# Second mixer (S5): rows on 128 partitions, turns by small diagonal products, copies shared between ScalarE and VectorE in another way

## The reference, cut to what matters

```python
h = modulate(rms_norm(x, norm1_g[layer]), sh1, sc1)        # latent rows
hc = modulate(rms_norm(ctx, norm1_g[layer]), sh1c, sc1c)   # context rows
...
def s5_mixer(h, hc, ...):            # 64 groups of 16 channels, 64 complex states per group
    ...
    for di, rev in enumerate((False, True)):
        yc_d, h_ctx = s5_scan(u_c, lam_bar, b_bar, c_mat, h0, rev, need_ctx)
        yl_d, _ = s5_scan(u, lam_bar, b_bar, c_mat, h_ctx, rev, True)
        y = y + yl_d
    z = gelu(y);  val, gt = split(z @ glu_w + glu_b);  return val * sigmoid(gt)
...
x = x + g1 * y
```

## Time and profile before

| | us |
|---|---|
| median of 3 runs | 2510.58 (2507.99 to 2512.06) |
| the profiled execution, its own time | 2506.16 |
| its span, first to last instruction | 2504.4 |
| mixer of the second layer, from its first transfer | 1461.3 |
| first turn of rows on PE (U) | 1501.4 |
| first product of V | 1515.9 |
| first context level of the recurrence | 1563.6 |
| first fill | 1606.4 |
| first GLU product | 1645.5 |

### The profile page before, as it was taken

How to read it: one execution, slowest core, us unless ns; L and a number is a source line. 1 busy time by engine, 2 the same in 40 slices (tenths; PEclk the granted TensorE clock), 3 DMA queues, 4 the chain that set the end, 5 groups by cost and what they waited for, 6 DMA issues and landing times. The chain is left out here.

```text
span 2504.4 us, 40476 instructions
## 1 busy us (share of the span) xinstructions
PE 2143.6 (86%) x11989; PEld 1189.9 (48%) x11990; DVE 1092.3 (44%) x2311; ACT 509.8 (20%) x945; POOL 433.9 (17%) x359
## 2 busy tenths in 40 slices
PE   5889999997999999999999816699789999988874
PEld 3765444744544444444444405354444444444442
DVE  8853365944543333333333338942532222222222
ACT  3443233611121111111111125220221111100000
POOL 1000000002012222222222210000122222232332
PEclk9999999998999999999999968799799999999997
DMA  9971002003799999999999669830499999899996
GB/s 358 386 265 46 34 34 84 1 1 131 264 346 355 354 358 357 359 351 350 355 358 358 202 158 329 275 146 0 160 404 375 361 363 358 274 390 372 385 385 207
DMA packets 173622, 666.72 MB, mean 266 GB/s; under 512 B 37666, under 2 KB 48898, under 8 KB 129882
## 3 DMA queue, kind: packets, MB, share of 16 engines
q1 hardware_dynamic: 121410, 564.71, 58.7%
q0 software_dynamic: 36160, 64.84, 11.0%
q10 hardware_dynamic: 15960, 35.96, 4.1%
HBM read 617.29 MB, written 86.09 MB: 281 GB/s over the span
## 5 line engine op out<-in xcount | busy, mean ns | idle before, releaser
L1518 PE MATMUL banks_l<-slotw_l,xTw_l 128*128 128x512 f32 x800 | 358.2, 601 | 27.7 <-issue 27.7
L1529 PE MATMUL banks_l<-slotn_l,xTn_l 128*64 128x256 f32 x2816 | 325.0, 383 | 34.5 <-issue 34.5
L1529 PEld LDWEIGHTS banks_l<-slotn_l,xTn_l 128*64 128x64 f32 x2816 | 212.0, 137 | 178.9 <-issue 104.8
L1518 PEld LDWEIGHTS banks_l<-slotw_l,xTw_l 128*128 128x128 f32 x800 | 148.5, 191 | 239.3 <-issue 239.3
L1568 PE MATMUL banks_l<-slotn_l,late_l 128*64 128x512 f32 x704 | 189.9, 615 | 19.6 <-DVE late_l L1356 17.9
L1547 PE MATMUL banks_l<-slotw_l,late_l 128*128 128x512 f32 x400 | 191.8, 602 | 15.4 <-DVE late_l L1338 15.4
L977 POOL DMA_INDIRECT xgw_l<-moe_h,idxw_l x58 | 60.6, 1045 | 741.0 <-PE banks_l L1463 367.1
L1005 POOL DMA_INDIRECT moe_acc<-late_l,idxn_l x88 | 151.2, 1718 | 190.5 <-DMA moe_acc<-late_l,idxn_l 172.5
L937 POOL IOTA slotw_l<- 128x1 f32 x2 | 0.3, 140 | 729.1 <-POOLq L69 431.3
L1335 DVE TENSOR_TENSOR late_l<-late_l,banks_l 128x256 f32<-128x256 f32 x50 | 21.0, 421 | 240.2 <-ACT late_l L1107 240.2
L556 PE MATMUL ps_a<-W_a,hT_a 128*128 128x512 f32 x288 | 124.9, 595 | 0.0
(11 more groups left out here) (433 smaller groups left out, 3235.0 us busy)
## 6 DMA issues: line engine op xcount, KB each, us to landing
slotn_l<-in_exp_w_gate SPq DMA_DIRECT2D x88, 1024.0 KB
slotn_l<-in_exp_w_up SPq DMA_DIRECT2D x88, 1024.0 KB
slotn_l<-in_exp_w_down SPq DMA_DIRECT2D x88, 1024.0 KB, 12.1
slotw_l<-in_exp_w_gate SPq DMA_DIRECT2D x50, 1024.0 KB
slotw_l<-in_exp_w_up SPq DMA_DIRECT2D x50, 1024.0 KB
slotw_l<-in_exp_w_down SPq DMA_DIRECT2D x50, 1024.0 KB
w_p<-in_mod_w SPq DMA_DIRECT2D x12, 2048.0 KB, 15.4
W_a<-in_ar_w_in SPq DMA_DIRECT2D x5, 2048.0 KB, 9.4
```

The costliest lines, as they stand in the source:

```text
L1518: last = pe.matmul(pGU_w, xT_w[b % 2][:, k, :], wgu[0][b % WIDE_RING][:, :, k, :], start=(k == 0), stop=(k == KD - 1))
L1529: last = pe.matmul(pGU_n[H * side:H * side + H, b % 2], xT_n[b % 2][:, k % 4, H * (k // 4):H * (k // 4) + H], w[:, :, k, P * side:P * side ...
```

## The change

- The rows lie on 128 partitions. A latent tile m (0 to 3) holds step m on partitions 0 to 63 and step m + 4 on 64 to 127, which is the shape of the residual tile. The first partial sum is therefore loaded into `x` itself (`XL`), the second into `ZU` (`XL1`). The 256 context rows fill two tiles of 128 partitions (`XC`, `XC1`; 4 steps by 32 chunks). There are six transfers of 128x1024 for each partial sum; sums, squares and scalings are six of 128x1024. The copy back into `x` and its semaphore `xres_in` are gone.
- ACT issues the `vec` loads first. All sixteen `s5_r` loads are SP's, and SP issues the first two modulation weights among them: w[1] ahead of the fourth, w[0] ahead of the sixth, behind a wait for all sums. ACT issues w[2] after its part of U.
- In U, each group's transpose is replaced by six products with the identity: two of 64x64 (latent halves) and four of 32x32 (context quarters), on the diagonal of the array.
- In V, ACT also makes the backward context copy of eleven of the sixteen half blocks; DVE makes it for 2, 5, 8, 11 and 14 only (`DVE_CTX`), and does whole sweeps between them.
- In the states stage ACT also copies the backward half of blocks 2, 4 and 6 (`ACT_BACK`).
- 65 tiny memsets in place of 50. The output rows are written with the new order of steps.

```diff
+        DVE_CTX = (2, 5, 8, 11, 14)
+        ACT_BACK = (2, 4, 6)
+        def evicted(hb):
+            return 3 * (hb + 1) - ctx_copied(hb)
+        def ctx_copied(hb):
+            return sum(k <= hb for k in DVE_CTX)
+        def lat_rows(part, m):
+            return part.rearrange("(h m c) d -> m h c d", m=NL, h=2)[m, :, 0:NCL, :]
+        def ctx_rows(part, r):
+            return part.rearrange("(q r c) d -> r q c d", q=4, r=2)[r, :, NCL:NCK, :]
...
-            for j in range(4):
-                sp.dma_start(X[:, 2 * j:2 * j + 2, :], parts[0].rearrange("(t c) d -> c t d", t=SL)[:, 2 * j:2 * j + 2, :])\
-                  .then_inc(x_in[j], 16)
-            for hb in range(R_ACT, NHB):
-                if hb == 4:
-                    sp.wait_ge(S['x_sum'], SL)
-                    for m in range(NL):
-                        for hh in range(2):
-                            sp.dma_start(x[hh * 64:hh * 64 + 64, m, :], X[0:64, 2 * m + hh, :]).then_inc(S['xres_in'], 16)
+            for m in range(NL):
+                sp.dma_start(XL[:, m, :], lat_rows(parts[0], m)).then_inc(x_in[m], 16)
+            for r in range(2):
+                sp.dma_start(XC[:, r, :], ctx_rows(parts[0], r)).then_inc(x_in[NL], 16)
+            for hb in range(NHB):
+                if hb == 3:
+                    sp.dma_start(w[1], mod_weights(io, *MOD_LATE[0], 1)).then_inc(m_in[1], 16)
+                if hb == 5:
+                    sp.wait_ge(S['x_sum'], NROW)
+                    sp.dma_start(w[0], mod_weights(io, *MOD_LATE[0], 0)).then_inc(m_in[0], 16)
...
+                if hb not in DVE_CTX:
+                    act.activation(VH[64:P, 0:NCC, :, gs].rearrange("p c a g -> p g a c"), v_of(hb)[64:P, :, :, 0:NCC], ACT.Copy)\
+                       .then_inc(S['va_done'], 1)
...
+                if b in ACT_BACK:
+                    act.activation(SV[64:P, :, g, :], VH[64:P, NCK - 2:NCC - 2:-1, :, g].rearrange("p c a g -> p a g c"),
+                                   ACT.Copy).then_inc(S['sf_done'], 1)
...
+            for b in range(NB):
+                for hb in (2 * b, 2 * b + 1):
+                    if hb in DVE_CTX:
+                        dve.wait_ge(S['va_done'], evicted(hb - 1) + 1)
+                        dve.tensor_copy(VH[64:P, 0:NCC, :, 4 * hb:4 * hb + 4].rearrange("p c a g -> p g a c"), v_of(hb)[64:P, :, :, 0:NCC])\
+                           .then_inc(S['vd_done'], 1)
                 for stage in range(4):
                     sweep(b, stage)
...
-                    last = pe.transpose(ps[:, at:at + NCK], Xn[:, gg].rearrange("p t j -> p (t j)"), ident[0:NCK, 0:NCK])
+                    for h in range(2):
+                        of = slice(64 * h, 64 * h + 64)
+                        pe.matmul(ps[of, at:at + NCL], XnL[of, gg].rearrange("p m j -> p (m j)"), ident[of, of],
+                                  start=True, stop=True, skip_group_check=True)
+                    for k in range(4):
+                        of = slice(32 * k, 32 * k + 32)
+                        last = pe.matmul(ps[of, at + NCL:at + NCK], XnC[of, gg].rearrange("p r j -> p (r j)"), ident[of, of],
+                                         start=True, stop=True, skip_group_check=True)
...
-            pe.wait_ge(S['va_done'], 2 * NHB)
-            pe.wait_ge(S['vd_done'], NHB)
+            pe.wait_ge(S['va_done'], evicted(NHB - 1))
+            pe.wait_ge(S['vd_done'], ctx_copied(NHB - 1))
```

More of the change, by code:

```diff
@@ L2025, in s5_mixer @@
     NCK = NCL + NCC
+    NROW = NL + 2
     x, cT = st['x'], st['cT']
@@ L2078, in s5_mixer @@
         S = {n: sem(n) for n in names.split()}
-        x_in = [sem(f"x_in{j}") for j in range(4)]
+        x_in = [sem(f"x_in{j}") for j in range(NL + 1)]
         r_in = [sem(f"r_in{b}") for b in range(len(Rflat))]
@@ L2194, in _ @@
             act.activation(warm[:], ident[0:1, 0:1], ACT.Sqrt).then_inc(S['warm'], 1)
[L2195 to L2200, removed]
+            for k in range(NROW):
+                act.wait_ge(S['x_sum'], k + 1)
+                if k:
+                    act.wait_ge(S['sq_done'], k)
+                act.activation(UV[:, 0:D], XL[:, k, :] if k < NL else XC[:, k - NL, :], ACT.Square,
+                               accum_out=ss[:, k:k + 1]).then_inc(S['sq_done'], 1)
             act.wait_ge(S['var_done'], 1)
@@ L2203, in _ @@
             act.wait_ge(S['sd_done'], 1)
-            for s in range(XN_DVE, SL):
-                act.activation(Xn[:, :, s, :], X[:, s, :].rearrange("p (g j) -> p g j", j=SI), ACT.Copy, scale=ss[:, s:s + 1])\
-                   .then_inc(S['xn_act'], 1)
+            act.activation(XnL[:, :, NL - 1, :], XL[:, NL - 1, :].rearrange("p (g j) -> p g j", j=SI), ACT.Copy,
+                           scale=ss[:, NL - 1:NL]).then_inc(S['xn_act'], 1)
+            act.activation(XnC[:, :, 1, :], XC[:, 1, :].rearrange("p (g j) -> p g j", j=SI), ACT.Copy,
+                           scale=ss[:, NROW - 1:NROW]).then_inc(S['xn_act'], 1)
             act.wait_ge(S['vec_done'], 1)
@@ L2215, in _ @@
                 last.then_inc(S['u_act'], 1)
-            act.wait_ge(S['xres_in'], 16 * 8)
-            for n in range(3):
-                act.dma_start(w[n], mod_weights(io, *MOD_LATE[n // 2], n % 2)).then_inc(m_in[n], 16)
+            act.dma_start(w[2], mod_weights(io, *MOD_LATE[1], 0)).then_inc(m_in[2], 16)
             for hb in range(NHB):
@@ L2267, in _, with sums @@
             done = Counter(dve, S['chain'])
[L2269 to L2272, removed]
+            def sums(m):
+                dve.wait_ge(x_in[m], 32 if m < NL else 64)
+                if m < NL:
+                    dve.tensor_tensor(XL[:, m, :], XL[:, m, :], XL1[:, m, :], ALU.add).then_inc(S['x_sum'], 1)
+                else:
+                    for r in range(2):
+                        dve.tensor_tensor(XC[:, r, :], XC[:, r, :], XC1[:, r, :], ALU.add).then_inc(S['x_sum'], 1)
             def squared(level):
@@ L2292, in _ @@
             dve.sem_inc(S['rep_done'], 1)
-            sums(1)
+            for m in (1, 2):
+                sums(m)
             dve.wait_ge(S['l8_in'], 16)
@@ L2419, in _ @@
                 dve.wait_ge(S['fill'], 4 * (b + 1))
-                states(b)
+                if b not in ACT_BACK:
+                    states(b)
             dve.wait_ge(S['o_mm'], NW)
@@ L2423, in _ @@
                 turned(b)
-            for _ in range(50):
+            for _ in range(65):
                 done(dve.memset(sqr[:, 0, 0, 0:1], 0.0))
@@ L2577, in x_final @@
             steps = out[0].rearrange("(c s) d -> s c d", s=SL)
-            return [(slice(64 * j, 64 * j + 64), steps[2 * t + j]) for j in range(2)]
+            return [(slice(64 * j, 64 * j + 64), steps[t + NL * j]) for j in range(2)]
         with ExitStack() as early:
```

80 lines of the change are left out of this document (37 added, 43 removed).

## The result

| | us |
|---|---|
| before, median of 4 runs | 2509.28 (2503.93 to 2512.06) |
| changed kernel, median of 4 runs | 2625.10 (2621.14 to 2626.17) |
| ratio, 95% interval | 1.0461 (1.0440 to 1.0483) |
| span of the profiled execution | 2619.4, before 2504.4 |

The account below looks back on a forecast made before the run. Bounds: front by poor-rate transfers, V by DVE, the fill by two nearly equal chains, DVE and transfer-bound modulation products. Front -12.5, U +20.5, V -2.5 gave +5.5 us: 2511.7 profiled, median 2516, range 2499 to 2531.

Parts of the forecast that it names:

- Front, -12.5: Up to the start of U: partial sums loaded on 128 partitions at 402 GB/s instead of 262, saving 12.5 us.
- My last rival: Front: partial-sum loads stay at 262 GB/s because of their source; front gives 2.5 us, sum +15.5, 2526; chance 0.06.
- the port rule: Front: each half of the partitions shares 8 of 16 ports, so 96 partitions get 0.75 of full rate; gain 9 us.
- U, +20.5: U: 64 groups of products that change size take 35 us in place of 14.5, a loss of 20.5 us.
- If it rises after 5 to 12 us: U: PE's clock leaves half speed after 5 to 12 us, so 8 to 17 groups run slowly, 0.24 us more each.
- my second rival: U: clock stays at half throughout, since products this short may not raise it; U +32.5, sum +17.5, 2528; chance 0.19.
- Size changes are cheap: U: rival in which changes of product size cost little; U +6, sum -9, 2501.6 us; chance 0.24.
- V, recurrence 40 us and T 36 us behind it: V: recurrence 39.8 us after V's start (was 47.6), T 36.3 (was 33.0); fill 2.5 us earlier against V.
- the transfers give back 3 to 5 us: Modulation chain behind T: transfers have less queued by then, which returns some 3 to 5 us of T's delay.
- States, 0: Fill to first GLU product: copies moved from DVE to ACT change nothing; first GLU product 39 us after the fill.
- my slow clock: U: rival with the clock at half throughout; U costs +32.5 us; chance 0.19.
- slow front: Front: rival with partial-sum loads still at 262 GB/s; the front gains only 2.5 us; chance 0.06.

Follow-up runs that it names:

- e8_rows_apart: The changed kernel with its partial-sum loads fetching rows 6 apart instead of neighbouring (wrong rows); U starts 32.5 us after the mixer's first instruction.
- e2_by_size: The changed kernel with loads cut where the source jumps and U's products grouped by size, 8 size changes in place of 128; 2522.69 us.
- e1_split: The changed kernel with each partial-sum load cut where its source jumps, latent loads in two, context loads in four; 2541.11 us, ratio 1.0126.
- e6_one_size: The changed kernel with loads cut where the source jumps and all turns of U at one size, a third more products; 2528.87 us.

## Why the prediction was wrong, point by point

- **Front, -12.5, came out at +85.9.** The step that failed is "On 128 partitions I take 402, the rate of rows of the same 4 KB": I took the rate from how a transfer's target looks and never looked at the source's outermost dimension, which the diff shows (2 and 4). With 2 of 16 engines it is 52 GB/s. My last rival named the source (chance 0.06, "because of their source"), though with 262 GB/s as the price, and I argued it away with "every load on 128 partitions from DRAM runs near 400", which these loads refute. With the loads cut the 402 fail a second time, at 238 to 266 GB/s. Here the cut took away what the 402 rested on, transfers of 128 partitions; that this is the cause is likely from the rows above but not shown, and the port rule that I had weighed stays open. And in e8_rows_apart 3.5 MB of other loads, not 0.9, share the way.
- **U, +20.5, came out at +31.3.** The price of a group was right: 0.455 us at full clock (0.45), 0.667 at half (0.69). The step that failed is "If it rises after 5 to 12 us": the clock was 0.50 throughout, which was my second rival (+32.5). Its reason, "products this short may not raise it", is wrong too: the same products by size raise it. "Size changes are cheap" is refuted.
- **V, recurrence 40 us and T 36 us behind it**: measured 40.2 and 36.4, and the last modulation product releases the fill, as told. The step that failed is that the transfers give back 3 to 5 us: the chain ended 91.1 us behind V instead of about 88.7, and -2.5 became +0.8. In the runs with T at 36 to 37 us the chain ended 89.1 to 91.1 us behind V, so part of this is spread, but none came to 88.7.
- **States, 0, came out at +1.9.** PE waits 2.46 us for the weights behind the GLU's 4 MB, a queue that I had not followed to its end.
- **Memsets**: 1.9 us under the GLU, as told. What they are for I missed; without the 15, e2_by_size took 35 us more. The forecast was spared only because the change had them.
- **The second expert stage, 0**: -4.9 us, from a clock that rose sooner.

With the loads cut the change costs 32 us (e1_split), which is close to my slow clock with a slow front: -2.5 + 32.5 - 2.5 = 27.5.

## What to carry to other kernels

Before the rate of a load is taken from its neighbours, read its access pattern: an outermost dimension of 2 or 4 leaves most transfer engines idle, and a DMA share of two or four sixteenths shows it at once. Look at how many partitions each single transfer fills, too: in the stretches shown here, transfers that filled all 128 with all engines at work ran at 369 to 410 GB/s, and the narrower ones at 200 to 266. Keep products of one tile size together on PE; each change costs time and, in a steady alternation, the clock. When the instructions of an engine become fewer ahead of a runtime loop, compare the packets of the instruction queue before any other explanation of a slower loop.

## What the runs showed of the hardware that I had not expected

- With all 16 transfer engines busy, transfers of 64 or 32 partitions ran at 238 to 266 GB/s from DRAM and at 200 inside the chip's memory. Transfers of 128 partitions ran at 400 with rows 24 KB apart, at 403 with rows 64 KB apart, and at 369 and 408 with rows side by side.
- While PE alternated between two 64x64 and four 32x32 products, the granted clock fell from 0.97 to 0.50 with PE busy 5.00 of 5 us, and stayed there for 36 us.
- Short products with few or no changes of size show a gap every 256 instructions of PE, 0.6 to 1.8 us in e2_by_size and up to 2.8 in e6_one_size.
- 11 instructions less on DVE ahead of a loop cost 38 us in it; the instruction queue moved 42 packets more in all.
